# Building the ten late one-hot blocks on VectorE instead of GpSimd in a transformer step with routed experts

## The chip, the cores and the metric

One Trainium2 chip, one core. The metric is the device time of one execution in microseconds (us), from runs of the same program; smaller is better. Engines are written as in the profile: PE (TensorE matmul) and PEld (its weight load), DVE (VectorE), ACT (ScalarE), POOL (GpSimd), SP (SyncE).

## The reference

One layer of a diffusion backbone over 640 tokens of width 1024 (512 latent tokens and 128 context tokens): modulated RMS norm, a mixer (differential attention and a short gated convolution), a residual, and then experts chosen per token. The change touches the experts alone:

```
# per token: best group of 4, then the best 2 of its 4 experts, with weights "gate"
for e in range(N_EXPERTS):            # 16 experts, width 512
    a = jax.nn.silu(t @ p['w_eg'][e]) * (t @ p['w_eu'][e])
    y = y + gate[:, e:e + 1] * (a @ p['w_ed'][e])
x = x + gate2 * rmsnorm(y, p['g_post2'])
```

Every token has two of the sixteen experts, so 1280 rows of expert output have to be added back into 640 token rows.

## The kernel before

**Tiles of rows.** The rows of each expert are cut into tiles of 128. The first tiles are one per expert, more tiles follow for experts with over 128 rows; they are worked off in pairs, (i, 2) and (i, 3), in a hardware loop whose count is read from the routing, after two tiles outside it. Behind the loop come the last two tiles, written out: (last, 2) and (last, 3). A third name, (last, 4), is only the turn in which the down weights of (last, 3) are split and used.

**Work of a tile.** All products are float32 products made of three float32r products: each operand is split in a high part (ACT casts it, L871 for weights) and a low part (DVE subtracts, `split_lo_moe`, L1388, 128x1024 at a time, four quarters each for gate weights (j = 0), up weights (j = 1), and the down weights of the tile before (j = 2)). PE multiplies gate and up (L2018), transposes the next tile's rows (L2001), multiplies down for the tile before (L2038) and transposes the activations (L2026). DVE also makes the low part of the transposed activations (`aT_lo`, L1488), the product with the silu (`gated`, L1495), and the low part of the next tile's rows (`xT_lo`, L1483). ACT copies each finished tile's output out of PSUM (L995) and starts its DMA to a DRAM buffer `expert_rows` (L999). SP loads the weights (L474), POOL gathers the rows of coming tiles with an indirect DMA (`next_rows`, L595 to L602).

**The last two tiles** are not written to DRAM. Their outputs, scaled, are split into `late_rows` (L1040 on ACT, L1589 on DVE), and PE adds them to the token rows by a product with a one-hot matrix (`late_add`, L2052). The one-hot blocks `late_oh` are 2 tiles x 5 token blocks = 10 blocks of 128x128. Block (q, b) is 1 where the count along the row (`count`) equals the token's place less 128 b (`last_place`, made by DVE ahead of the loop, L1561, signalled by `early_ready`). PE waits for ten increments of the semaphore `late_oh` (L2101) only behind its very last down product.

**The end of POOL's program.** After the last `next_rows` POOL makes the ten blocks (L630 to L634). Then it waits (L635 to L640), among other things for the second up quarter of tile (last, 3) to be split, and for all tile outputs to have landed in `expert_rows`. A one-element addition (L641) stands ahead of ten indirect gathers (L643 to L647), which bring the rows of the earlier tiles back, two per token block, the second choice first. The gathers' rows go through ACT (`gated_row`, L1046) and DVE (`row_sum`, L1585), the late products are added, and each token block is normalised and written out.

**Order.** Each engine works its own instructions strictly in the order written; there is no planner. Across engines there are only semaphores.

Of the kernel before, what the change touches and what calls it, by code (L numbers as in the profile page):

```python
# [25 lines left out]
ALU = mybir.AluOpType  # L26
# [3 lines left out]
P = 128  # L30
# [3 lines left out]
TB = (L_LAT + L_CTX) // P  # L34
# [28 lines left out]
def build(nc, a):  # L63
# [16 lines left out]
    with ctx:  # L80
        def sb(name, shape, dt=F32):
            return ctx.enter_context(nc.sbuf_tensor(name, shape, dt))
# [195 lines left out]
        def lin(tile, a, b):  # L278
            i, c = tile
            return a * c + b if i is None else i * (2 * a) + (a * c + b)  # L280
# [7 lines left out]
        def moe_split(tile, j, r, part):  # L288
            if tile[0] is None and tile[1] == 0 and j == 0 and r < 2:
                return hs[:, part, (3 + r) * D:(4 + r) * D]  # L290
            return spl[:, moe_split_slot(tile, j, r), part, :]

        def moe_raw(tile, j, r):
            n = pos(tile, j, r) % MOE_RAW
            if n < 4:
                return qkv[:, 2048 + 1024 * n:3072 + 1024 * n]
            if n < 8:
                return raw[:, n - 4, :]
            o = (0, 1024, 6144, 7168)[n - 8]
            return qkv[:, o:o + 1024]  # L300
# [5 lines left out]
        def moe_lo(tile, j, r):  # L306
            n = PRE_S + pos(tile, j, r) + 1
            return n if tile[0] is None else tile[0] * 24 + n
# [18 lines left out]
        late_oh = [hs[:, q, 2048:2688] for q in range(2)]  # L327
# [3 lines left out]
        last_place = small[:, 40:50].rearrange("p (q b) -> p q b", q=2)  # L331
# [12 lines left out]
        count = sb("token_count", [P, P])[:, :]  # L344
# [178 lines left out]
        def _(pool):  # L523
# [104 lines left out]
                next_rows((i, 4))  # L628
            next_rows((last, 3))
            pool.wait_ge(S["early_ready"], 1)  # L630
            for q in range(2):
                for b in range(TB):
                    pool.tensor_scalar(late_oh[q][:, b * P:(b + 1) * P], count, last_place[:, q, b:b + 1], None, ALU.is_equal
                                       ).then_inc(S["late_oh"], 1)  # L634
            for b in ADDED:  # L635
                pool.wait_ge(x_in[b], 48)
            pool.wait_ge(S["xs_tr"], lin((last, 3), 1, 1))
# [439 lines left out]
        def _(dve):  # L1077
# [7 lines left out]
            tt, ts, stt = nc.vector.tensor_tensor, nc.vector.tensor_scalar, nc.vector.scalar_tensor_tensor  # L1085
# [299 lines left out]
            def split_lo_moe(tile, j, quarters=range(4)):  # L1385
                for r in quarters:
                    dve.wait_ge(S["hi"], moe_lo(tile, j, r))
                    tt(moe_split(tile, j, r, 1), moe_raw(tile, j, r), moe_split(tile, j, r, 0).bitcast(F32), ALU.subtract).then_inc(S["lo"], 1)  # L1388
# [97 lines left out]
            def aT_lo(tile):  # L1486
                dve.wait_ge(S["aT_ev"], lin(tile, 1, 1))
                tt(hs[:, 1, 1024:1536], ps[:, 4, :], hs[:, 0, 1024:1536].bitcast(F32), ALU.subtract).then_inc(S["aT_lo"], 1)  # L1488
# [81 lines left out]
            expert_tile((last, 2))  # L1570
            split_lo_moe((last, 3), 0)
            aT_lo((last, 2))
            split_lo_moe((last, 3), 1)
            split_lo_moe((last, 3), 2)
            gated((last, 3))
# [582 lines left out]
```

## Time and profile before

| what | value |
|---|---|
| device time, 3 runs | median 684.89 us (684.49 to 685.68) |
| the profiled execution | 689.32 us, its span 687.6 us |
| mean granted PE clock | 0.989 of full speed |
| busy in the span | PE 656.3, PEld 526.9, DVE 520.5, ACT 416.5, POOL 102.3 us |
| instructions on POOL / DVE | 150 / 756 |
| HBM traffic | 166.12 MB read, 21.53 MB written |

The profiled execution is some 4.4 us longer than the median of the runs without a profile. Its span runs from the first to the last instruction; all starts in rows are counted from there. Rows of the timeline have start, duration, engine, line, operation, the memory written and read, the count of instructions merged into the row, and in brackets the idle time ahead of it with what ended it.

### The profile page before, as it was taken

How to read it: one execution, taken by the hardware profiler on the slowest of the kernel's cores; microseconds unless marked ns; L12 is line 12 of the kernel's file. 1: busy time of each engine (PE TensorE's matmuls, PEld its weight loads, DVE VectorE, ACT ScalarE, POOL GpSimd, SP SyncE). 2: the span in 40 equal slices, each digit the busy share in tenths (PEclk: the TensorE clock that was granted, in tenths of full speed). 3: DMA queues.
4: the chain of work that ended last, by engine and by line, in shares of the span. 5: the costliest groups of instructions: out<-in, count | busy, mean ns of one | idle time of the engine just before them, and what ended most of it. 6: DMA issues, size and time to landing. Idle time of an engine off the chain costs nothing.

```text
span 687.6 us, 10864 instructions
## 1 busy us (share of the span) xinstructions
PE 656.3 (95%) x3492; PEld 526.9 (77%) x3492; DVE 520.5 (76%) x756; ACT 416.5 (61%) x629; POOL 102.3 (15%) x150
## 2 busy tenths in 40 slices
PE   3999999999999999999989899999999999999983
PEld 0577767789999987778838688888888888888861
DVE  2667798656446468766579899999999999999966
ACT  5552222244434559884444578888888888888953
POOL 2030001055000000000013200000000000370361
PEclk9999999999999999999989999999999999999997
DMA  9975876539321243006798999999999999999586
GB/s 327 354 257 190 285 240 190 166 101 378 94 80 60 93 153 118 6 1 211 280 337 305 345 367 412 411 412 412 412 412 411 412 411 412 412 412 411 225 278 153
DMA packets 79002, 188.15 MB, mean 274 GB/s; under 512 B 7619, under 2 KB 29176, under 8 KB 78964
## 3 DMA queue, kind: packets, MB, share of 16 engines
q1 hardware_dynamic: 67456, 153.11, 60.3%
q0 software_dynamic: 7200, 22.47, 9.8%
q10 hardware_dynamic: 4310, 12.10, 4.4%
q8 instruction: 21, 0.34, 0.2%
q14 instruction: 15, 0.12, 0.1%
HBM read 166.12 MB, written 21.53 MB: 273 GB/s over the span
## 4 chain that ended last, share of the span: by engine, by line
PE 83%; DVE 6%; DMA 4%; SPq 2%; POOL 2%; issue 1%; ACT 1%; ACTq 0%; POOLq 0%; DVEq 0%
PE ps L2018 22%; PE ps L2038 11%; PE ps L1783 10%; PE ps L1843 8%; PE ps L1811 8%; PE ps L1815 5%; PE ps L1886 3%; PE ps L1716 3%; PE ps L1861 2%; PE ps L2001 2%; PE ps L1877 2%; SPq L403 2%; PE ps L1941 1%; DMA qkv_mem<-in_w_mod 1%; DMA catT_mem<-token_rows,token_lists 1%
## 5 line engine op out<-in xcount | busy, mean ns | idle before, releaser
L2018 PE MATMUL ps<-split_ring,split_rows 128*128 128x512 f32 x756 | 176.1, 392 | 1.2 <-DVE split_rows L1483 1.0
L2018 PEld LDWEIGHTS ps<-split_ring,split_rows 128*128 128x128 f32 x756 | 140.7, 188 | 30.5 <-DVE split_rows L1483 1.2
L1388 DVE TENSOR_TENSOR split_ring<-qkv_mem,split_ring 128x1024 fp32r<-128x1024 f32 x126 | 146.2, 1220 | 21.9 <-ACT split_ring L871 21.9
L871 ACT CAST split_ring<-qkv_mem 128x1024 fp32r<-128x1024 f32 x126 | 123.5, 1056 | 13.0 <-ACT catT_mem L995 9.2
L2038 PE MATMUL ps<-split_ring,split_rows 128*128 128x512 f32 x360 | 86.0, 394 | 0.0
L1811 PE MATMUL ps<-split_rows,split_ring 128*128 128x384 f32 x288 | 85.7, 345 | 0.2
L1815 PE MATMUL ps<-split_rows,split_ring 128*128 128x256 f32 x288 | 77.0, 280 | 0.0
L2038 PEld LDWEIGHTS ps<-split_ring,split_rows 128*128 128x128 f32 x360 | 66.5, 188 | 13.3
L1388 DVE TENSOR_TENSOR split_ring<-raw_ring,split_ring 128x1024 fp32r<-128x1024 f32 x64 | 74.2, 1221 | 0.0
L1783 PE MATMUL ps<-split_ring,split_rows 128*128 128x512 f32 x288 | 68.2, 393 | 0.0
L871 ACT CAST split_ring<-raw_ring 128x1024 fp32r<-128x1024 f32 x64 | 62.5, 1049 | 1.7 <-DMA raw_ring<-in_w_exp_up 1.7
L1783 PEld LDWEIGHTS ps<-split_ring,split_rows 128*128 128x128 f32 x288 | 53.3, 188 | 11.6 <-issue 0.9
L688 ACT CAST split_ring<-raw_ring 128x1024 fp32r<-128x1024 f32 (+1 forms) x36 | 34.1, 957 | 44.5 <-DMA raw_ring<-in_w_in 36.5
L1843 PE MATMUL ps<-split_ring,split_rows 128*128 128x512 f32 x240 | 60.6, 400 | 0.0
L1811 PEld LDWEIGHTS ps<-split_rows,split_ring 128*128 128x128 f32 x288 | 53.2, 188 | 1.7 <-issue 1.4
L1815 PEld LDWEIGHTS ps<-split_rows,split_ring 128*128 128x128 f32 x288 | 53.3, 188 | 0.0
L1843 PEld LDWEIGHTS ps<-split_ring,split_rows 128*128 128x128 f32 x240 | 43.4, 188 | 8.2
L1109 DVE TENSOR_TENSOR split_ring<-raw_ring,split_ring 128x1024 fp32r<-128x1024 f32 (+1 forms) x36 | 39.6, 1101 | 10.9 <-ACT split_ring L688 10.6
L1244 DVE TENSOR_REDUCE small<-ps 128x1 f32<-128x640 f32 (+1 forms) x40 | 26.8, 712 | 15.0 <-PE ps L1867 7.8
L983 ACT CAST split_rows<-ps 128x512 fp32r<-128x512 f32 x32 | 17.3, 588 | 32.7 <-PE ps L2001 26.6
L599 POOL TENSOR_TENSOR rows_now<-token_lists 128x1 uint32<-128x1 uint32 x13 | 5.5, 420 | 192.7 <-PE ps L2001 192.7
L1211 DVE SCALAR_TENSOR_TENSOR catT_mem<-raw_ring,cond_columns,catT_mem 128x512 f32<-128x512 f32 x42 | 31.5, 750 | 1.2
(350 smaller groups left out, 928.0 us busy)
## 6 DMA issues: line engine op xcount, KB each, us to landing
qkv_mem<-in_w_exp_gate SPq DMA_DIRECT2D x64, 512.0 KB, 9.5
qkv_mem<-in_w_exp_up SPq DMA_DIRECT2D x60, 512.0 KB, 7.9
raw_ring<-in_w_exp_down SPq DMA_DIRECT2D x60, 512.0 KB, 9.5
raw_ring<-in_w_mod SPq DMA_DIRECT2D x28, 512.0 KB, 4.8
qkv_mem<-in_w_mod SPq DMA_DIRECT2D x32, 256.0 KB, 7.8
expert_rows<-catT_mem ACTq DMA_DIRECT2D x14, 512.0 KB, 6.7
expert_rows<-work POOLq DMA_DIRECT2D x26, 256.0 KB, 6.7
raw_ring<-in_w_in SPq DMA_DIRECT2D x12, 512.0 KB, 8.1
```

The source lines that it names most:

```text
L688: nc.scalar.copy(spl[:, (4 * n + r) % SPLIT, 0, 0:m], raw[:, q % RAW, 0:m]).then_inc(S["hi"], 1)
L871: nc.scalar.copy(moe_split(tile, j, r, 0), moe_raw(tile, j, r)).then_inc(S["hi"], 1)
L1109: tt(spl[:, slot, 1, 0:m], raw[:, rslot, 0:m], spl[:, slot, 0, 0:m].bitcast(F32), ALU.subtract).then_inc(S["lo"], 1)
L1211: ins = ts(total, w, s, None, ALU.mult) if k == 0 else stt(total, w, s, total, ALU.mult, ALU.add)
L1244: nc.vector.reduce_max(nm[:, u % 2, c:c + 1], psf[:, SC[c]:SC[c] + nk], axis=AX, negate=True).then_inc(S["neg_max"], 1)
L1388: tt(moe_split(tile, j, r, 1), moe_raw(tile, j, r), moe_split(tile, j, r, 0).bitcast(F32), ALU.subtract).then_inc(S["lo"], 1)
L1783: ins = mm(ps[:, g % 2, :], hS[:, s, k, b * P:(b + 1) * P], weight(n, k, m), start=(k == 0 and s + m == 0), stop=(k == KC - 1 and s == 1))
L1811: return mm(ps[:, CONV_BANK, 0:LOW], conv_weight(n, k, s, part), hS[:, m, k, 0:LOW], start=(k == 0 and s + m == 0), stop=(k == KC - 1 and ...
L1815: return mm(ps[:, CONV_BANK + 1, 0:HIGH], conv_weight(n, k, s, part), hS[:, m, k, LOW:TOK], start=(k == 0 and s + m == 0), stop=(k == KC - ...
L1843: ins = mm(ps[:, banks + j, :], cS[:, s, b, kk, :], weight(place["o", j], kk, m), start=(kk == 0 and s + m == 0), stop=(kk == KC - 1 and s ...
L2018: ins = mm(ps[:, j, :], xS[:, s, k, :], moe_split(tile, j, k // 2, m)[:, (k % 2) * N:(k % 2 + 1) * N], start=(k == 0 and s + m == 0), stop ...
L2038: ins = mm(ps[:, 5 + half, :], aS[:, s, k, :], spl[:, moe_split_slot(turn, j, k), m, half * N:(half + 1) * N], start=(k == 0 and s + m == ...
```

## The change

The ten comparisons leave POOL's program and enter DVE's, between `aT_lo((last, 2))` and the split of the up weights of tile (last, 3). The wait on `early_ready` moves with them. Operands, output, comparison and semaphore increments stay; `ts` is DVE's `tensor_scalar`. Nothing else changes.

```diff
@@ POOL, after next_rows((last, 3)) @@
             pool.wait_ge(S["early_ready"], 1)
-            for q in range(2):
-                for b in range(TB):
-                    pool.tensor_scalar(late_oh[q][:, b * P:(b + 1) * P], count, last_place[:, q, b:b + 1], None, ALU.is_equal
-                                       ).then_inc(S["late_oh"], 1)
             for b in ADDED:
                 pool.wait_ge(x_in[b], 48)
@@ DVE @@
             expert_tile((last, 2))
             split_lo_moe((last, 3), 0)
             aT_lo((last, 2))
+            dve.wait_ge(S["early_ready"], 1)
+            for q in range(2):
+                for b in range(TB):
+                    ts(late_oh[q][:, b * P:(b + 1) * P], count, last_place[:, q, b:b + 1], None, ALU.is_equal
+                       ).then_inc(S["late_oh"], 1)
             split_lo_moe((last, 3), 1)
             split_lo_moe((last, 3), 2)
             gated((last, 3))
```

## Rows read from the trace of the kernel before

**Rows 1.** The page: busy time by engine, and the chain that ended last.
```profile
PE 656.3 (95%) x3492; PEld 526.9 (77%) x3492; DVE 520.5 (76%) x756; ACT 416.5 (61%) x629; POOL 102.3 (15%) x150
PE 83%; DVE 6%; DMA 4%; SPq 2%; POOL 2%; issue 1%; ACT 1%; ACTq 0%; POOLq 0%; DVEq 0%
```

**Rows 2.** Busy time by stretch, one tile each: with POOL's ten blocks, and without.
```profile
601.00:618.70 17.70, 17.70 (x86) 14.79 (x85) 16.26 (x17) 14.56 (x17) 13.40 (x8) 1.00 1.03 412
618.70:636.40 17.70, 17.70 (x86) 14.79 (x85) 16.31 (x17) 14.57 (x17) 0.00 (x0) 1.00 1.03 411
```

**Rows 3.** Timeline of POOL from the ten blocks to the fifth gather.
```profile
597.53 16.88 POOL L633 TENSOR_SCALAR split_rows<-token_count,small 128x128 fp32r<-128x128 f32 x10
645.63 3.58 POOL L641 TENSOR_TENSOR small<-small 128x1 f32<-128x1 f32 x1 [31.23 <-DMA expert_rows<-catT_mem]
649.50 1.03 POOL L645 DMA_INDIRECT catT_mem<-expert_rows,early_slots  x1 [0.28 <-POOL small L641]
650.83 2.03 POOL L645 DMA_INDIRECT catT_mem<-expert_rows,early_slots  x1 [0.31 <-issue]
653.16 2.56 POOL L645 DMA_INDIRECT catT_mem<-expert_rows,early_slots  x1 [0.30 <-issue]
656.02 0.94 POOL L645 DMA_INDIRECT catT_mem<-expert_rows,early_slots  x1 [0.30 <-issue]
657.26 1.63 POOL L645 DMA_INDIRECT x_rows<-expert_rows,early_slots  x1 [0.30 <-issue]
```

**Rows 4.** The chain that ended last, in order of time: start, length, what.
```profile
638.45 7.04 DMA expert_rows<-catT_mem
...
659.20 5.57 DMA catT_mem<-expert_rows,early_slots
...
664.86 1.30 DVE catT_mem L1585
```

**Rows 5.** Timeline of DVE, around the place of the change and behind it.
```profile
604.56 4.73 DVE L1388 TENSOR_TENSOR split_ring<-qkv_mem,split_ring 128x1024 fp32r<-128x1024 f32 x4 [1.44 <-ACT split_ring L871]
...
637.77 0.68 DVE L1488 TENSOR_TENSOR split_rows<-ps,split_rows 128x512 fp32r<-128x512 f32 x1
639.99 4.63 DVE L1388 TENSOR_TENSOR split_ring<-qkv_mem,split_ring 128x1024 fp32r<-128x1024 f32 x4 [1.53 <-ACT split_ring L871]
644.54 4.63 DVE L1388 TENSOR_TENSOR split_ring<-raw_ring,split_ring 128x1024 fp32r<-128x1024 f32 x4
649.08 0.69 DVE L1495 TENSOR_TENSOR qkv_mem<-ps,work 128x512 f32<-128x512 f32 x1
649.68 2.35 DVE L1388 TENSOR_TENSOR split_ring<-qkv_mem,split_ring 128x1024 fp32r<-128x1024 f32 x2
...
652.55 2.35 DVE L1388 TENSOR_TENSOR split_ring<-qkv_mem,split_ring 128x1024 fp32r<-128x1024 f32 x2
...
656.80 1.28 DVE L1585 SCALAR_TENSOR_TENSOR catT_mem<-catT_mem,small 128x1024 f32<-128x1024 f32 x1 [0.67 <-DMA catT_mem<-expert_rows,early_slots]
```

**Rows 6.** Timeline of DVE at its own ten 128x128 comparisons, and what follows them.
```profile
371.95 2.04 DVE L1529 TENSOR_SCALAR split_rows<-token_count,work 128x128 fp32r<-128x128 f32 x10
373.91 0.68 DVE L1483 TENSOR_TENSOR split_rows<-ps,split_rows 128x512 fp32r<-128x512 f32 x1
```

**Rows 7.** Timeline of DVE, two operations where each waits for the one before.
```profile
362.42 0.24 DVE L1465 TENSOR_TENSOR work<-work 128x80 f32<-128x80 f32 x1
362.69 0.24 DVE L1466 SCALAR_TENSOR_TENSOR work<-work 128x80 f32<-128x80 f32 x1
```

**Rows 8.** Timeline of PEld and PE around and behind the place of the change.
```profile
649.98 0.59 PEld L2026 LDWEIGHTS ps<-ident,qkv_mem 128*128 128x128 f32 x4
...
636.50 11.15 PE L2018 MATMUL ps<-split_ring,split_rows 128*128 128x512 f32 x48
...
650.21 0.60 PE L2026 MATMUL ps<-ident,qkv_mem 128*128 128x128 f32 x4
...
663.26 3.94 PE L2055 MATMUL ps<-split_ring,split_rows 128*128 128x512 f32 x16 [2.43 <-DVE split_ring L1589]
```

## The prediction

> **What bounds the kernel now.** I read the page's busy times and chain first: PE is busy 95% of the span and holds 83% of the chain, POOL 15% and 2% [rows 1]. So work is only worth something where it stands on PE's way or on the short piece of chain that is not PE's. Next I looked at the two neighbouring tiles by stretch. While POOL made most of its ten blocks and in the next tile, when it made none, PE was busy 17.70 of 17.70 us both times [rows 2]. The third view is the chain in order of time. From 638.45 us on PE is off it. It goes through the DMA of the last tile output to DRAM (7.04 us), POOL's tiny addition L641, the issues of five gathers, the sixth from its issue at 659.20 to its landing (5.57 us), and then DVE's row sum at 664.86 [rows 4]. The fourth view is POOL beside DVE in that stretch, and there lies the point of this change.
>
> L641 adds one element per partition and took 3.58 us, from 645.63 to 649.21 [rows 3]. Over that time DVE ran a closed series of L1388 subtractions, which ended at 644.54 + 4.63 = 649.17 [rows 5]. POOL's gathers show the same. The fourth, which met no such operation at its end, took 0.94 us. The second ended at 650.83 + 2.03 = 652.86, which is 0.83 behind the end of DVE's pair (649.68 + 2.35 = 652.03). The third ended at 655.72, which is 0.82 behind 654.90, the end of the next pair. The fifth ended at 658.89, 0.81 behind 658.08, the end of the first row sum [rows 3, 5]. So POOL's instructions here end when DVE's operations with two SBUF operands let them. **POOL's chain hangs on the times of DVE**, although DVE itself is hardly on the chain before 664.86.
>
> **The change, part by part.** *Removed from POOL:* ten comparisons, 16.88 us from 597.53 to 614.41. Behind them POOL was idle for 31.23 us, until the DMA of the last output had landed [rows 3]. That DMA is started by ACT behind PE and knows nothing of POOL. The removal brings POOL nothing. It might give DVE something back: in that stretch four subtractions took 4.73 us where four took 4.63 later, but they stood behind an idle 1.44 us, in which DVE waited for ACT, and PE had no gap [rows 5, 2]. I take 0; the gain is excluded because DVE's wait swallows it.
>
> *The wait on `early_ready`:* it is signalled by DVE itself ahead of its loop. It costs nothing beyond one sequencer step. Behind it stand all of DVE's last splits, so it would matter if it were not met, and it always is.
>
> *Added to DVE:* ten comparisons of 128x128. DVE has done the same operation ten times at 371.95: `count` against a column, to float32r. The next instruction started 373.91, so the ten advanced the engine by 1.96 us, 0.196 each [rows 6]. Those ten had one increment in all, the new ones have one each. The L1388 subtractions have an increment each and still overlap: four take 4.63 us and two 2.35, so each further one adds 1.14, while one alone is 2.35 - 1.14 = 1.21 [rows 5]. I take 1.96.
>
> *The cover:* `aT_lo((last, 2))` starts at 637.77 and lets the next instruction start 0.60 later, at 638.37, as L1495 of the same size does (649.08 to 649.68) [rows 5]. With 1.96 us the comparisons are through at 640.33. The first up subtraction began at 639.99 before, after 1.53 us of waiting for ACT's cast [rows 5]. So the hole takes 1.6 us and **DVE is late by 0.34 us**. From there to 654.90 DVE has no idle time that could take it back: eight quarters, `gated`, four quarters and the last `aT_lo` follow each other directly.
>
> *What the lateness does on PE:* the product `gated` was done at 649.77, and PE loaded for its transposes at 649.98 [rows 5, 8]. With 0.34 it is done at 650.11, so PE starts these some 0.15 to 0.2 us late. The first up quarter lands at 640.33 + 1.22 = 641.55. PE's 48 gate and up products run for 11.15 us from 636.50 [rows 8]; the up half starts half way, at about 642.0, its weights some 0.2 earlier as L2026's (649.98 and 650.21), which just holds. PE later stood idle for 2.43 us at 663.26, waiting for DVE [rows 8], so a loss of 0.2 us there costs nothing.
>
> *What it does on POOL:* L641 is released at the end of the series, 649.51 in place of 649.17, and the first gather starts 0.34 later. The second and third end behind DVE's pairs, which are 0.34 later too, and the fifth behind the first row sum, which itself waited for the second gather [rows 5]. All keep their places against each other, and the sixth gather starts 0.34 later at 659.54. Its landing and the row sums, squares and outputs behind it follow. **Sum:** 0 + 0 + 0.34 = +0.34 us on the profiled span of 687.6, and the same on the median of 684.89, some 685.2.
>
> A rule of the Trainium skill, "SBUF — State Buffer", section "Who interferes with whom", speaks otherwise on how long POOL waits: a VectorE instruction with two SBUF inputs holds back a GpSimd one that reads SBUF, and whoever comes first has the ports for that one instruction. By the rule's letter L641 would have run at the end of the one subtraction that it met. The trace disagrees, since it waited for four in a row; by the rule DVE's lateness would not pass whole to POOL, which is the second case below.
>
> **Bounds of the unknown.** What an increment per comparison costs is not in [rows 6]. At least nothing: if the ten took 1.62 us or less they would fit in the hole and the sum is 0. At most each waits for the end of the one before, as where operations wait for each other: 0.24 us of work every 0.27, 0.03 on top [rows 7]. The comparisons last 2.04 - 9 x 0.196 = 0.28 us singly, so 0.31 each, 3.1 in all, DVE late by 638.37 + 3.1 - 639.99 = 1.5 us. I take the low price since L1388 overlaps with its increments.
>
> **The rivals.**
> 1. *The lateness is lost on the way, no change:* POOL's addition is let in at some other boundary of DVE's series, or the gathers' landings are set by the DMA engines and not by their issue. Against it: three gathers and L641 all end at DVE's ends within 0.02 us of a constant. Gives 684.9.
> 2. *Slower, the comparisons run one by one on DVE:* the upper bound above. The first up quarter would land at 641.5 + 1.2 = 642.7, 0.7 after PE wants it, L641 would end 1.5 later, and the end with it: 684.89 + 1.5 = 686.4. It decides by over 0.2% from 0.30 us per comparison. Against it: the ten of [rows 6], and the overlap of L1388.
> 3. *Faster, POOL's addition escapes the series:* were L641 to take 0.2 us in place of 3.58, all gathers would start up to 3.4 us earlier, about 681.5 to 683 after what DVE's pairs still hold. For it only: timing behind 645.63 moves. Against it: DVE's series becomes later, not thinner, and covers 640.33 to 649.51 without a hole.
> 4. *The change does not do what it says in time*, as POOL's 16.88 us were covered by 31.23 idle: this is part of the forecast, not against it.
>
> **How the numbers follow.** About 0.2%, 1.4 us, is what a measurement of this kernel can tell from no change; the three runs spread over 1.2. Forecast (+0.2 to +0.6): 0.62. Rival 1: 0.24, also within the bound. Rival 2: 0.07, and 0.01 for other losses above 1.4 us. Rival 3: 0.05 with what else may gain; 0.01 is left. Same = 0.87, slower 0.08, faster 0.05. The range goes from rival 1 less the spread of runs, 684.4, to the forecast plus that spread and short of the upper bound, 686.2.
>
> **What the next profile would show.** Ten comparisons on DVE between 638.4 and 640.4, about 2.0 us merged, and none on POOL behind 597. No wait for ACT before the first up quarter, which starts near 640.33. L641 again long, and ending 0.04 behind DVE's `raw_ring` series, near 649.5. PE's L2026 some 0.2 late, PE's 2.43 idle a little changed. The forecast is wrong if that first quarter starts beyond 640.7, if L641 ends well away from the series, or if the sixth gather has not moved with DVE.

## The result, and the profile after

| comparison with the kernel before | this, median | before, median | ratio, 95% interval |
|---|---|---|---|
| the changed kernel, 4 executions of each | 690.46 us (689.25 to 691.75) | 685.28 us (684.49 to 685.78) | 1.0077 [1.0055, 1.0098] |
| again on another occasion (n2) | 690.91 us, 8 runs | 686.43 us, 25 runs | 1.0056 [1.0037, 1.0075] |

The change makes the kernel slower by 4.5 to 5.2 us by the medians. (For n2 the quotient of the medians is 1.0065, within the interval of its ratio.) The forecast was +0.3 us, with 686.2 as the upper end. Yet the profile after looks like the profile before: span 687.5 against 687.6 us. That contradiction is where the explanation starts, so here is what answers to [rows 3] and [rows 5]. First DVE's timeline of the changed kernel (start, duration, engine, line, operation; lines are four lower for the split):

```profile
637.11 0.69 DVE L1484 TENSOR_TENSOR split_rows<-ps,split_rows 128x512 fp32r<-128x512 f32 x1
637.71 2.04 DVE L1572 TENSOR_SCALAR split_rows<-token_count,small 128x128 fp32r<-128x128 f32 x10
639.67 4.63 DVE L1384 TENSOR_TENSOR split_ring<-qkv_mem,split_ring 128x1024 fp32r<-128x1024 f32 x4
644.21 4.63 DVE L1384 TENSOR_TENSOR split_ring<-raw_ring,split_ring 128x1024 fp32r<-128x1024 f32 x4
```

The ten comparisons advance DVE by 1.96 us (637.71 to 639.67), exactly as taken from [rows 6], although each now has a semaphore increment. The wait for ACT ahead of the up split is gone. From L1484's start to the first up subtraction it is 2.56 us, against 2.22 in [rows 5]: late by 0.34, as forecast. Then POOL's timeline:

```profile
644.47 4.42 POOL L637 TENSOR_TENSOR small<-small 128x1 f32<-128x1 f32 x1 [47.64 <-DMA expert_rows<-catT_mem]
...
650.41 2.11 POOL L641 DMA_INDIRECT catT_mem<-expert_rows,early_slots  x1 [0.31 <-issue]
652.82 2.57 POOL L641 DMA_INDIRECT catT_mem<-expert_rows,early_slots  x1 [0.30 <-issue]
```

The one-element addition (L641 before, L637 now; "the addition" from here on) ends at 648.89, 0.05 behind DVE's series (644.21 + 4.63 = 648.84). This, too, is the picture of the kernel before in [rows 3]. Every step of the forecast is there. So either the comparison of times misleads, or the trace of before was not the usual execution.

### The profile page after: what moved, and what is told of

It is laid out like the page before. It is cut to its first block, busy times and chain, and to the rows that moved or that the text cites. A ratio compares the mean times of both kernels' runs of the same rounds, so it can differ in the third digit from the quotient of the medians.

```text
span 687.5 us, 10865 instructions
## 1 busy us (share of the span) xinstructions
PE 657.0 (96%) x3492; PEld 527.7 (77%) x3492; DVE 521.9 (76%) x766; ACT 416.9 (61%) x629; POOL 87.3 (13%) x140
## 4 chain that ended last, share of the span: by engine, by line
PE 84%; DVE 5%; DMA 4%; SPq 2%; POOL 1%; issue 1%; ACT 1%; ACTq 0%; DVEq 0%; POOLq 0%
PE ps L2019 23%; PE ps L2039 11%; PE ps L1784 9%; PE ps L1812 8%; PE ps L1844 7%; PE ps L1816 5%; PE ps L1717 3%; PE ps L1887 2%; PE ps L1862 2%; PE ps L2002 2%; PE ps L1878 2%; SPq L403 2%; PE ps L2056 1%; PE ps L1942 1%; DMA qkv_mem<-in_w_mod 1%
## 5 line engine op out<-in xcount | busy, mean ns | idle before, releaser
L1105 DVE TENSOR_TENSOR split_ring<-raw_ring,split_ring 128x1024 fp32r<-128x1024 f32 (+1 forms) x36 | 39.5, 1101 | 11.8 <-ACT split_ring L684 11.6
L765 ACT ACTIVATE x_rows<-ps,small 128x640 f32<-128x640 f32 (+1 forms) x40 | 28.1, 712 | 4.2 <-DVE small L1240 4.2
```

The costliest lines, as they stand in the source:

```text
L765: nc.scalar.activation(out[:, 0:nk], psf[:, SC[c]:SC[c] + nk], ACT.Exp, bias=nm[:, u % 2, c:c + 1], accum_out=sm[:, u, c:c + 1]).then_inc( ...
L1105: tt(spl[:, slot, 1, 0:m], raw[:, rslot, 0:m], spl[:, slot, 0, 0:m].bitcast(F32), ALU.subtract).then_inc(S["lo"], 1)
```

## The experiments

All but n3 and n4 were timed with 8 to 12 runs each, beside 17 to 35 runs of the kernel before in each group, whose medians were 686.3 to 686.8 us.

**n1: the kernel before again.** No edit.

> The kernel before against itself. If the measured 1.0077 is a property of the changed kernel, this ratio is within 0.2% of 1 (0.998 to 1.002) on this chip. If it comes from how the compared executions were taken or from the chip, this run is also some 4 to 5 us (0.6% or more) above the kernel before, although it is the same program.

Measured: median 685.44 us, ratio 0.9983 [0.9962, 1.0003], so the kernel before is no slower when it is measured again, and the 5 us stay. Its profile (span 683.8 us) differs from the first one of the same program. POOL's timeline, and DVE's:

```profile
644.93 1.12 POOL L641 TENSOR_TENSOR small<-small 128x1 f32<-128x1 f32 x1 [31.42 <-DVE split_ring L1388]
...
649.60 1.22 POOL L645 DMA_INDIRECT catT_mem<-expert_rows,early_slots  x1 [0.30 <-issue]
```

```profile
639.10 4.63 DVE L1388 TENSOR_TENSOR split_ring<-qkv_mem,split_ring 128x1024 fp32r<-128x1024 f32 x4 [1.54 <-ACT split_ring L871]
643.65 4.62 DVE L1388 TENSOR_TENSOR split_ring<-raw_ring,split_ring 128x1024 fp32r<-128x1024 f32 x4
...
648.78 2.35 DVE L1388 TENSOR_TENSOR split_ring<-qkv_mem,split_ring 128x1024 fp32r<-128x1024 f32 x2
```

DVE's series is the same, step for step, but the addition takes 1.12 us and ends at 646.05. The subtractions advance by 1.14 us each, so the third starts about 645.93: POOL was let in between two of them. The third gather ended at 650.82, 0.8 behind the end of the first subtraction of its pair (648.78 + 1.22 = 650.00), where in [rows 3, 5] it ended 0.82 behind the end of a whole pair (the next pair, as it was later there). So there are two ways it can go: **let in** (POOL gets its turn at the next boundary between subtractions) and **held** (POOL waits until the whole series is over).

**n2: the changed kernel again.** No edit.

> The changed kernel again, beside the kernel before on one chip. Theory A (the first comparison set executions of two kinds or two chips against each other; the two traces have spans of 687.5 and 687.6 us): ratio within 0.999 to 1.001, my forecast of +0.34 us being 1.0005. Theory B (the change itself costs 5 us, in something that a trace hides): ratio 1.006 to 1.009 again, and n1 at 1.

Measured: 690.91 us, ratio 1.0056, as theory B said. The profile shows the addition held again, 4.22 us.

**e1: comparisons ahead of the loop.** Against the changed kernel:

```diff
             expert_tile((None, 1))
+            dve.wait_ge(S["early_ready"], 1)
+            for q in range(2):
+                for b in range(TB):
+                    ts(late_oh[q][:, b * P:(b + 1) * P], count, last_place[:, q, b:b + 1], None, ALU.is_equal
+                       ).then_inc(S["late_oh"], 1)
...
             aT_lo((last, 2))
-            dve.wait_ge(S["early_ready"], 1)
-            for q in range(2):
-                for b in range(TB):
-                    ts(late_oh[q][:, b * P:(b + 1) * P], count, last_place[:, q, b:b + 1], None, ALU.is_equal
-                       ).then_inc(S["late_oh"], 1)
             split_lo_moe((last, 3), 1)
```

> The ten comparisons on DVE, but ahead of the loop, behind the tile (None, 1); none in the last tiles and none on POOL. Theory A: the same time as n2 and the kernel before, within 0.2%, and 0.3 us under n2 at most, since DVE's last splits are no longer late. Theory B with the place as cause: back to ratio 1.000. Theory B with the missing POOL work as cause (POOL idle for 47 us ahead of the gathers): as slow as n2, 1.006 to 1.009.

Measured: 686.12 us, ratio 0.9991 [0.9973, 1.0009]; the addition took 0.19 us. POOL has no comparisons here either, and the loss is gone. So it is the place on DVE, not the work that POOL no longer has.

**e2: ten dummies on DVE, POOL keeps its own.** DVE computes ten comparisons for nothing, into unused memory (`spare`). Against the kernel before:

```diff
             aT_lo((last, 2))
+            for n in range(10):
+                ts(spare[n], count, last_place[:, n // TB, n % TB:n % TB + 1], None, ALU.is_equal)
             split_lo_moe((last, 3), 1)
```

> The kernel before, POOL's ten comparisons kept, and ten more of the same (to unused memory) on DVE at the place of the change: extra work that is computed for nothing. Theory P (it is the place on DVE that costs: DVE's series of two-input subtractions starts 0.35 us later with no wait for ACT in it, and POOL's L641 is then held to the end of the series, 3.6 to 4.4 us, in every execution): as slow as the changed kernel, 690 to 692 us, ratio 1.005 to 1.008, L641 at 3.5 us or more. Rival Q (it is POOL's missing work that costs): like the kernel before, ratio 1.000, L641 held in some executions only.

Measured: 690.07 us, ratio 1.0057 [1.0038, 1.0076]; addition 3.74 us, held. The loss comes back with POOL's work in place. Theory P stands, Q falls.

**e3: five ahead of the loop, five at the place.** The diff is that of e1 with q = 0 moved and q = 1 left.

> The changed kernel, but five of the ten comparisons ahead of the loop and five at the place of the change: 5 x 0.196 = 0.98 us, which fits in DVE's 1.5 us of waiting for ACT, so the series starts when it did before. Theory P: like the kernel before, ratio 0.998 to 1.002, L641 0.2 to 1.2 us in most executions. Rival R (comparisons at that place do it by being there, whatever their length): 1.005 to 1.008.

Measured: 685.95 us, ratio 0.9995 [0.9975, 1.0014]; DVE waited 0.55 us for ACT, the addition took 0.20 us.

**e4 and e5: gaps in the series,** in the changed kernel and in the kernel before.

```diff
-            split_lo_moe((last, 3), 2)
+            for r in range(4):
+                split_lo_moe((last, 3), 2, (r,))
+                if r < 3:
+                    nc.vector.memset(work[:, 1152 + r:1153 + r], 0.0)
             gated((last, 3))
```

One such memset also stands inside each of the two pairs of (last, 4), five in all.

> The changed kernel with a one-element DVE memset, which reads no SBUF, between the subtractions of the last down splits (five in all). If L641 and the gathers are held because the two-input subtractions follow each other without a gap, POOL gets in at the first such memset: L641 under 1.4 us, the third gather under 1.5 us, and the time falls by 2 to 4 us against the changed kernel, to 686 to 688. If the hold has another cause, the time stays at 690 to 692 or rises by the memsets' 0.5 us.

> The kernel before with the same five memsets. If gaps let POOL in: its executions above 688 us are gone and it is as fast as the kernel before or 0.5 to 1.5 us faster in the median (684.5 to 686). If not: unchanged, with the same spread from 684 to 689.

Measured: e4 686.85 us, ratio 1.0003 [0.9983, 1.0023]; e5 686.25 us, 0.9999 [0.998, 1.0017]. POOL and DVE in e4:

```profile
646.14 0.31 POOL L637 TENSOR_TENSOR small<-small 128x1 f32<-128x1 f32 x1 [48.34 <-DMA expert_rows<-catT_mem]
```

```profile
638.68 2.05 DVE L1572 TENSOR_SCALAR split_rows<-token_count,small 128x128 fp32r<-128x128 f32 x10
640.63 4.63 DVE L1384 TENSOR_TENSOR split_ring<-qkv_mem,split_ring 128x1024 fp32r<-128x1024 f32 x4
645.17 2.37 DVE L1384 TENSOR_TENSOR split_ring<-raw_ring,split_ring 128x1024 fp32r<-128x1024 f32 x2
646.35 0.06 DVE L1578 MEMSET work<- 128x1 f32 x1
```

The comparisons stand where the change put them and DVE does not wait for ACT, but the addition ends at 646.45, a tenth behind the start of the first memset. Five instructions of 0.06 us bring 4 us back (n2 is 4.5 us over its kernel before, e4 0.5). So the hold of POOL is the loss. In the kernel before the memsets gain nothing: e5's runs still spread from 684.7 to 688.2 us, so the hold is not all that spreads them, against my expectation.

**e6 and e7: a later request,** in the changed kernel and in the kernel before. Theory F: it matters when the addition asks, against DVE's series.

```diff
-            pool.wait_ge(S["lo"], moe_lo((last, 3), 1, 1))
+            pool.wait_ge(S["lo"], moe_lo((last, 3), 2, 0))
```

> The changed kernel, and POOL waits one series later ahead of L641: for the first quarter of the last down split (lo of (last, 3), 2, 0) in place of the second up quarter. That quarter ends 1.2 us into the series, so L641 asks later than it did (0.3 to 0.5 us into the series), right behind a boundary. Theory F (what decides is when L641's request falls against DVE's series: before its first boundary it is held to the end, behind it it is let in at the next boundary): L641 at 1.1 to 1.2 us instead of 4.2, over 2 us earlier, time 686 to 688.5 although a wait was added. Rival G (what decides is that DVE's series no longer had a wait for ACT in front): L641 held to the end of the series again (3.4 us), 690 to 692.

> The kernel before with the same later wait. Theory F: all executions like its faster ones, 684 to 686.5, with none at 688 to 689.6; median 0 to 1.5 us below the kernel before. Rival G: unchanged spread.

Measured: e6 689.74 us, 1.0044 [1.0025, 1.0064]; e7 686.09 us, 0.9992 [0.9965, 1.0019]. The two additions, e6 and then e7, each with the series that it met:

```profile
643.36 4.63 DVE L1384 TENSOR_TENSOR split_ring<-raw_ring,split_ring 128x1024 fp32r<-128x1024 f32 x4
...
644.81 3.23 POOL L637 TENSOR_TENSOR small<-small 128x1 f32<-128x1 f32 x1 [48.84 <-DVE split_ring L1384]
```

```profile
645.31 4.62 DVE L1388 TENSOR_TENSOR split_ring<-raw_ring,split_ring 128x1024 fp32r<-128x1024 f32 x4
...
646.76 0.96 POOL L641 TENSOR_TENSOR small<-small 128x1 f32<-128x1 f32 x1 [31.59 <-DVE split_ring L1388]
```

Both ask 1.45 us into the series. One is held to its end (648.04 against 647.99), one is let in at the next boundary. Theory F falls. What still differs on DVE is what came before: in e7 it had waited for ACT ahead of the up series, in e6 it had not (theory G). With that goes a second difference, which no run takes apart from the first: a DVE that did not wait runs further behind ACT's casts (below, at e8 and e13).

**e8, e13, e9: eight, nine and sixteen dummies** in e2's loop.

> The kernel before with eight added comparisons on DVE at the place of the change (for nothing, to unused memory): 8 x 0.196 = 1.57 us, which nearly fills the 1.6 us hole but does not make the series late. Both F and G: like the kernel before, ratio 0.998 to 1.002. If the presence of such work alone is the cause, 1.005 to 1.008.

> The kernel before with nine comparisons added on DVE (for nothing, to unused memory), one more than in e8: 9 x 0.196 = 1.76 us, which overfills the 1.6 us hole by 0.15. Theory G: DVE no longer waits for ACT, so L641 is held to the end of the series (3 us or more), 688.5 to 691.5, ratio 1.003 to 1.007, although only 0.2 us of work was added to e8. If the cause is graded and not a switch: within 0.2 us of e8, 686 to 687.

> The same with sixteen: 3.14 us, DVE 1.5 us late, 1.2 us more than with ten. Theory F: L641's request now falls ahead of the series, into the one before, and is held still longer or let in there; if held to the end, 691 to 692.5; if let in, 685 to 688. Rival G: held to the end, 691 to 692.5. PE waits up to 0.9 us for the first up quarter.

| dummies | wait for ACT left | the addition | median | ratio |
|---|---|---|---|---|
| 8 (e8) | 0.05 us | 0.72 us, let in | 686.17 us | 0.999 [0.9966, 1.0014] |
| 9 (e13) | none | 4.29 us, held | 689.69 us | 1.0045 [1.0027, 1.0062] |
| 10 (e2) | none | 3.74 us, held | 690.07 us | 1.0057 [1.0038, 1.0076] |
| 16 (e9) | none | 5.47 us, held | 690.73 us | 1.0052 [1.0028, 1.0075] |

The 0.05 us of e8 are 639.99 less 638.37 + 8 x 0.196. ACT's casts of the up weights and DVE in e8, and then in e13:

```profile
638.91 3.90 ACT L871 CAST split_ring<-qkv_mem 128x1024 fp32r<-128x1024 f32 x4 [0.62 <-ACT catT_mem L995]
638.37 1.46 DVE L1577 TENSOR_SCALAR work<-token_count,small 128x128 f32<-128x128 f32 x7
...
639.99 4.63 DVE L1388 TENSOR_TENSOR split_ring<-qkv_mem,split_ring 128x1024 fp32r<-128x1024 f32 x4
```

```profile
638.70 3.90 ACT L871 CAST split_ring<-qkv_mem 128x1024 fp32r<-128x1024 f32 x4 [0.63 <-ACT catT_mem L995]
638.16 1.46 DVE L1577 TENSOR_SCALAR work<-token_count,small 128x128 f32<-128x128 f32 x7
...
639.93 4.62 DVE L1388 TENSOR_TENSOR split_ring<-qkv_mem,split_ring 128x1024 fp32r<-128x1024 f32 x4
```

One comparison of 0.2 us more costs 3.5 us. It is a switch. In e8 DVE's up series starts 1.08 us behind ACT's, in e13 1.23. The distance lasts: at the down series it is 1.34 and 1.49 us. It is 1.34 to 1.35 in every profile in which DVE had waited, and 1.49 (e13) to 2.85 (e9) in every held one but the first profile of before, which has 1.34 (e4, with 1.66 and no wait, was let in with its memsets). So these runs do not tell whether the wait itself decides or the distance, with a threshold between these two. In e9 PE did wait for the first up quarter (0.58 us at 642.52), and its median is only 0.7 us above that of e2, although the stretch measured in the table further down is 1.8 us longer in its profile; PE stood idle 2.90 us later on, waiting for DVE.

**e10: the wait restored, the series late.** ACT copies 128x512 for nothing ahead of its up casts, in the changed kernel.

```diff
             out_rows((last, 1))
+            nc.scalar.copy(work[:, 1152:1664], x[:, 0, 0:N])
             split_expert((last, 3), 1)
```

> The changed kernel with one more 128x512 copy on ACT (of x to unused memory, for nothing, about 0.5 us) ahead of its casts of the last up weights. DVE's series then waits for ACT again, some 0.15 us, although it starts even later than in the changed kernel (0.5 against 0.34 us behind the kernel before). Theory G (a series that waited for ACT lets POOL in, one that did not holds it): L641 under 1.3 us, time 685 to 688 although both engines do more. Theory H (lateness itself, of the series or against the DMA, decides): L641 held over 3 us, 690 to 692.

Measured: 687.12 us, ratio 1.0003 [0.9976, 1.003]. POOL and DVE:

```profile
646.12 0.45 POOL L637 TENSOR_TENSOR small<-small 128x1 f32<-128x1 f32 x1 [48.31 <-DMA expert_rows<-catT_mem]
```

```profile
638.68 2.04 DVE L1573 TENSOR_SCALAR split_rows<-token_count,small 128x128 fp32r<-128x128 f32 x10
640.75 4.63 DVE L1385 TENSOR_TENSOR split_ring<-qkv_mem,split_ring 128x1024 fp32r<-128x1024 f32 x4
```

The series now starts 2.07 us behind the comparisons in place of 1.96, so DVE waited 0.1 us, and POOL is let in. It has more work on ACT than the changed kernel and as much on DVE, and it is over 3 us faster. Theory H falls. Theory G stands, and so does the distance as its rival: the down series starts 1.34 us behind ACT's again.

**e11: behind the splits.** The ten stand ahead of `row_sum(0)`.

> The ten comparisons on DVE behind late_lo(0), ahead of the first row sum, where DVE waits for a gather; POOL makes none. Theory G: DVE's last split series is as in the kernel before, so 685 to 687.5; the ten delay the first row sum by up to 1.3 us in an execution where L641 is let in early (the gathers are there sooner), which the next wait for a gather takes up. Theory H gives the same. Rival (POOL's missing work matters after all): 690 to 692.

Measured: 686.35 us, ratio 1.0 [0.9978, 1.0022]; addition 0.32 us.

**e12: e1 and the memsets of e5 together.**

> The ten comparisons ahead of the loop, and the five memsets between the last subtractions: a version meant to be faster than both. If the memsets remove the held executions and nothing else is lost, median 684.5 to 685.8, ratio to the kernel before 0.997 to 0.999. If e4 and e5 are typical (gathers seven and eight are held longer by row sums then), no better than the kernel before, 0.999 to 1.001.

Measured: 686.31 us, ratio 0.9996 [0.9976, 1.0017]. No gain: no version beat the kernel before.

**n3, n4: the kernel before, two more profiles.**

> The kernel before, one look at whether L641 is held in this execution. Theory G in its strict form says let in (under 1.3 us), since DVE waits for ACT in it; the first profile of this kernel, held at 3.58 us, contradicts that already, so a share of such executions is expected.

> As n3, a second look: let in, under 1.3 us, or held at 3 us or more as in the first profile.

Measured: 687.42 and 684.7 us; additions 0.58 and 1.28 us, both let in.

## Why the prediction was wrong

**All profiles together.** From the start of ACT's last output DMA to the start of DVE's last operation:

| | profiles | the addition | DMA start to last DVE start |
|---|---|---|---|
| DVE waited for ACT (all but e4) or had the memsets (e4, e5, e12): n1, n3, n4, e1, e3, e4, e5, e7, e8, e10, e11, e12 | 12, all let in | 0.19 to 1.28 us | 38.4 to 39.5 us |
| it did not wait: after, n2, e2, e6, e13 (and e9) | 6, all held | 3.23 to 5.47 us | 42.1 to 42.8 us (e9 44.5) |
| the first profile of before, waited | 1, held | 3.58 us | 42.2 us |

By these rows the hold costs some 3.5 us (on average 42.6 without e9 less 39.1). The medians of the held versions are 2.9 us (e13) to 5.2 us (the first comparison) over their kernel before. What the first comparison has beyond the hold and the 0.34 us of lateness is not explained.

- *Bounds by PE, removal free, comparisons 0.196 us each, DVE late by 0.34 us, PE unharmed:* right as far as the profiles show. Against the held execution of before, the stretch above is 42.75 against 42.18 us, 0.57 more, of which 0.34 was forecast.
- *POOL's addition and gathers hang on DVE's series:* right as a mechanism. But the rows bore less than I put on them. The second gather asked at 650.83, when the last subtraction of its pair had begun at 650.81 (652.03 less 1.22), and the fifth met a single row sum. Only L641 and the third gather show POOL held over a boundary.
- **The step that failed:** "the sixth gather starts 0.34 later ... and the same on the median of 684.89". I took the hold for a fixed part of the kernel before, since the one trace showed it, and so priced the filled wait at its lateness alone. In 11 of the 12 profiles in which DVE had waited for ACT, POOL was let in (without e5 and e12, which also had the memsets, 9 of 10; the one left over is the first profile). Of the four profiles of the kernel before one was held; of those in which the wait was filled, without memsets, six of six. So the term that was missing is the turn from let in to held, some 3.5 us, which I had at nothing. How often the kernel before is held the plain times do not say: 33 of the 142 runs of it beside the other versions took 688 us or more, and so did 23 of the 108 runs of the versions whose profile was let in. The warning stood in the table ahead of the prediction: the profiled execution was 689.32 us against 684.49 to 685.68 of the runs. I noted the gap and drew nothing from it; but n1's profiled execution, of the same program, took 685.53 us, in the middle of its runs.
- *Rival 1 (lateness lost)* did not happen. *Rival 2 (comparisons one by one)* had the right sign for a wrong reason: they overlap. *Rival 3* described the addition escaping the series as a gain that the change might bring; it was what the kernel before did in three of four profiles, and what the change took away.
- *The rule of the Trainium skill* that I set aside was nearer to the typical execution than my trace. In n1, e7 and the other let-in profiles the addition waits for one subtraction at most, as the Trainium skill, "SBUF — State Buffer", section "Who interferes with whom", says of VectorE instructions with two SBUF inputs. In the held ones it waits for three (e6) to five (e9) in a row; there the measurement differs, as it did in my trace.

**What stays open.** Why a DVE that has waited once, if only 0.05 us, lets POOL in at boundaries 5 and more us later, and one that has not does not. The subtractions have the same lengths and overlaps in both; what the profiles show to differ is their distance to ACT's casts, and no run changed that without the wait. Why the first profile of before was held although DVE had waited. And the rest of the spread of let-in executions: e11's profile is let in, its last DVE operation starts 39.35 us behind the DMA, and its span is still 686.8 us, since the output writes land late (10.0 us for one, against 7.0 in the first profile of before); the runs were not enough to say how often.

## What to carry to other kernels

Compare the profiled execution with the plain runs before pricing anything: a trace 0.5% above the slowest run may show a wait that most executions do not have. An idle stretch on VectorE is not free to fill just because VectorE is off the critical path: here filling 1.53 us of it cost 4.5 to 5.2 us, through GpSimd's chain of gathers at the end of the kernel. Where such a chain stands beside a series of two-input VectorE operations, place the work elsewhere (e1, e11), or break the series with a one-element memset (e4).

## What the runs showed of the hardware that was not expected

- A GpSimd instruction on one element per partition took 0.19 to 0.2 us at its shortest, up to 1.28 us when let in between VectorE's two-input subtractions of 1.22 us, and 3.2 to 5.5 us when held behind a closed series of them. GpSimd's ten comparisons of 128x128 in the kernel before took 0.59 us each at the shortest and 2.37 in the median, VectorE's 0.28.
- The issue of an indirect DMA on GpSimd depends on these subtractions too: 0.94 us free, 2.11 and 2.57 us in the changed kernel.
- One comparison of 0.2 us more ahead of the series, which ended VectorE's wait, switched between let in and held (e8 against e13: 3.5 us of time).
